# Four edits to a streaming-encoder layer with a mixture of experts: gathered rows spread over both partition halves, router products ahead of a gathered column, tile sums and additions interleaved, the output gain spread by products

## The chip, the cores and the metric

One core of a Trainium2 chip runs the whole program. Times are microseconds (us) on the device; the metric is the time of the whole program. Engines are called PE (TensorE), DVE (VectorE), ACT (ScalarE), POOL (GpSimd) and SP (SyncE, which here only issues DMAs). Sixteen DMA engines serve the core.

## What is computed

```
h = rmsnorm(concat(meta_tokens, x)); u = h @ w_in            # 16 + 512 rows of 1024
y = concat(conv_module(u), windowed_attention(u), hgrn2(u))
h_res = concat(meta_tokens, x) + y @ w_out
x2 = rmsnorm(h_res)                                          # ffn_norm
g = argmax(x2 @ w_rg + b_rg)                                 # 1 of 4 groups
e1, e2 = top2((x2 @ w_re + b_re)[group g])                   # 2 of its 8 experts, weights w1, w2
moe = sum over e in (e1, e2) of w_e * (silu(x2 @ w_gate[e]) * (x2 @ w_up[e])) @ w_down[e]
out = rmsnorm(h_res + moe)[16:]                              # final_norm, output (1, 512, 1024)
```

There are 32 experts. The three matrices of one expert are 1 MB each in float32, so the experts' weights alone are 96 MB.

## The kernel before, in words

The program is written engine by engine; semaphores order them. It has two stages. The mixer stage (to about 275 us) makes h_res for four tiles of 128 tokens. Its end interleaves the output projection with the router: `project` (L1516) makes a tile half, `router_turn` (L1524) turns 128x128 blocks of it, `router` (L1532) multiplies them with the router's weights, and DVE's `residual` (L953), `router_half` (L967, copies the turned half) and `select` (L985 to L1029) choose the experts. Line L960 writes the normed rows.

The expert stage works on **columns**: up to 128 rows of tokens, gathered by one indirect DMA into 128 partitions (`rows_in`, L2115), and scattered to `expert_out` by another one when their results are there (`rows_out`, L2121). A column holds one to four experts. `rows_plan` (L52) lays them out: six experts with low numbers start early ("early" columns, and "rest" columns for their rows of the last tile), the others are sorted by their count into heavy (one expert in 128 rows), mid (two in 64 rows each) and light columns (four in 32 rows each). Each part is a **block**: 42 in all. A block is gate and up products (L1628 for 64 rows, L1636 for 32), a silu on ACT (L1775, L1777), a product on DVE, a transposition (L1642, L1645), down products (L1651, L1659), and copies to `yb` by ACT and DVE (L1864 and others). `turn_x` (L1621) turns a gathered column for the products. PE's order is written out by block number in `experts_tensor`, DVE's in `experts_vector`.

SP loads the weights into a ring of seven slots, three DMAs an expert (L438, L441, L448), each issued when the products that read the slot are done. `places` (L1194) works out the row of each token in its column from a code word: two bits give the quarter (`rq`) at which its block starts, and `from_end` (quarters 1 and 2) says that the rows are counted down from the block's end:

```
mark(V.tensor_tensor(from_end, low_q, high_q, ALU.not_equal))
mark(V.tensor_scalar(row_r, cq, 32.0, -1.0, ALU.mult, ALU.add))
mark(V.scalar_tensor_tensor(out=row_r, in0=rq, scalar=64.0, in1=row_r, op0=ALU.mult, op1=ALU.add))
```

The index of a row that no token has lies beyond the bounds, and nothing is moved for it. With the given inputs the router's choices give these columns, in the order of the plan (counted from the reference's own top-2 choices; p is the partition):

| column | rows in p 0-63 | in p 64-127 |
|---|---|---|
| rest 13 | 19 | 0 |
| mid 4, light 8 | 36, 55 | 45, 49 |
| heavy 0, heavy 1 | 64, 64 | 22, 5 |
| light 9, heavy 2 | 46, 59 | 30, 0 |
| mid 5, heavy 3 | 36, 55 | 35, 0 |
| mid 6, mid 7 | 34, 30 | 32, 28 |
| light 11, light 10 | 5, 28 | 0, 17 |

Rest 12 is not gathered but picked from the last tile by products, and the last column, light 10, is not scattered: its results go into the sum by eight products (`last_rows`, L2009) whose weights `mix_flat` are made at blocks 20 to 25.

At the end (`rows_back`, L1689 and L1691) SP waits for all scatters and reads back, tile by tile, the residual rows and two expert rows for each token, 512 KB each. DVE's `two_rows` (L1903) adds the two weighted expert rows of a tile; then eight additions (L1913, two a tile) add the products of the last column; ACT squares and sums a tile (L1828), and `row_norm` (L1934) scales it. `gain_out` holds final_norm in all 128 partitions: POOL loads it with a broadcasting DMA (L2149) after the scatter of column number 9 of the plan. It cannot come sooner, since `slot_is` uses that memory until `last_rows` (L1258) has made `mix`.

## Time and profile before

| | |
|---|---|
| median of 3 runs | 553.11 us (552.26 to 555.14) |
| profiled execution, its own time | 553.58 us |
| its span | 551.7 us |
| PE busy, PE weight loads | 501.0 us (91%), 320.2 us (58%) |
| DVE, ACT, POOL busy | 255.5 us (46%), 154.1 us (28%), 39.0 us (7%) |
| moved by DMA | 146.71 MB, mean 266 GB/s |
| chain that ended last | PE 72%, DMA 16%, DVE 4%, SP's queue 4% |

The share of busy time is an average over two stages with different limits, so it has to be read by stretches. A DMA share slightly over 1 means that all 16 engines are occupied all the time.

### The profile page before, as it was taken

To read this page: it belongs to the slowest core of one execution; us is meant where nothing else is said; L and a number is where in the kernel's file an instruction comes from. 1 tells how busy PE (TensorE), PEld (TensorE's weight loads), DVE (VectorE), ACT (ScalarE), POOL (GpSimd) and SP (SyncE) were. 2 spreads that over 40 slices of the span, in tenths; PEclk is the share of its full clock that TensorE was granted. 3 is DMA by queue.
4 is the path that set the end of the run, shared out by engine and by line. 5 is a ranking of instruction groups with operands and counts; after the bars stand their busy time and mean duration, and the time that the engine had idled before them with its cause. 6 is when DMAs were issued, how large, how long until landed. Compare 5 with 4: busy or idle time off the path is not lost.

```text
span 551.7 us, 11100 instructions
## 1 busy us (share of the span) xinstructions
PE 501.0 (91%) x4585; PEld 320.2 (58%) x4585; DVE 255.5 (46%) x638; ACT 154.1 (28%) x380; POOL 39.0 (7%) x46
## 2 busy tenths in 40 slices
PE   5999999999999999999899999999999799776660
PEld 4886468885556655557566656565565455443420
DVE  3205995868245864626456333342442122131167
ACT  5410003766013622422123322231222111120124
POOL 0010000000001000000110011211111111000000
PEclk8899999999999999999979999999999899786885
DMA  8990000000006799607968899999999999999943
GB/s 268 363 350 3 1 0 2 0 1 1 2 1 215 266 421 410 264 39 266 400 229 337 351 407 336 414 413 418 417 413 413 417 416 416 420 416 411 404 166 152
DMA packets 38947, 146.71 MB, mean 266 GB/s; under 512 B 5151, under 2 KB 12565, under 8 KB 30320
## 3 DMA queue, kind: packets, MB, share of 16 engines
q1 hardware_dynamic: 32736, 134.18, 62.1%
q0 software_dynamic: 5616, 11.36, 5.6%
q8 instruction: 37, 0.61, 0.4%
q10 hardware_dynamic: 544, 0.44, 0.2%
q14 instruction: 14, 0.11, 0.1%
HBM read 135.83 MB, written 18.87 MB: 280 GB/s over the span
## 4 chain that ended last, share of the span: by engine, by line
PE 72%; DMA 16%; DVE 4%; SPq 4%; issue 1%; ACT 0%; DVEq 0%; POOLq 0%; ACTq 0%
PE bank L1628 10%; PE bank L1516 9%; PE bank L1347 6%; PE bank L1381 5%; DMA area_w<-in_w_exp_up 5%; PE bank L1349 5%; PE bank L1636 5%; PE bank L1651 5%; DMA area_x<-in_w_exp_up 4%; PE bank L1339 4%; DMA area_g<-expert_out 3%; PE bank L1460 3%; PE bank L1282 3%; PE bank L1621 2%; PE bank L1659 2%; PE bank L1423 2%
## 5 line engine op out<-in xcount | busy, mean ns | idle before, releaser
L1516 PE MATMUL bank<-area_w,area_m 128*128 128x512 f32 x128 | 56.7, 594 | 0.4 <-issue 0.4
L1628 PE MATMUL bank<-area_w,area_m 128*64 128x256 f32 x320 | 41.1, 403 | 3.3 <-DMA area_w<-in_w_exp_up 3.3
L785 DVE SCALAR_TENSOR_TENSOR area_m<-area_g,cols,area_m 128x512 f32<-128x512 f32 x60 | 39.8, 746 | 0.0
L1516 PEld LDWEIGHTS bank<-area_w,area_m 128*128 128x128 f32 x128 | 23.6, 190 | 26.9 <-issue 26.9
L1347 PE MATMUL bank<-area_h,area_w 128*128 128x264 f32 x160 | 35.9, 386 | 0.0
L1628 PE MATMUL bank<-area_g,area_m 128*64 128x256 f32 x256 | 32.8, 400 | 3.3 <-DMA area_g<-in_w_exp_up 3.3
L1628 PEld LDWEIGHTS bank<-area_w,area_m 128*64 128x64 f32 x320 | 23.0, 145 | 19.5 <-issue 9.8
L1347 PEld LDWEIGHTS bank<-area_h,area_w 128*128 128x128 f32 x160 | 30.4, 190 | 5.6 <-issue 0.5
L1381 PE MATMUL bank<-area_h,area_w 128*128 128x512 f32 x64 | 30.8, 612 | 0.0
L1846 DVE COPY cst<-bank 128x128 f32<-128x128 f32 (+1 forms) x38 | 9.9, 261 | 40.2 <-PE bank L1642 30.0
L1349 PE MATMUL bank<-area_h,area_w 128*128 128x512 f32 x64 | 27.6, 592 | 0.0
L1628 PEld LDWEIGHTS bank<-area_g,area_m 128*64 128x64 f32 x256 | 18.0, 142 | 15.8 <-issue 7.7
L1636 PE MATMUL bank<-area_g,area_m 128*32 128x128 f32 x640 | 23.2, 291 | 3.3 <-DMA area_g<-in_w_exp_up 3.3
L1864 DVE COPY area_m<-bank 64x512 f32<-64x512 f32 x20 | 13.9, 694 | 21.9 <-PE bank L1651 21.9
L1636 PEld LDWEIGHTS bank<-area_g,area_m 128*32 128x32 f32 x640 | 18.7, 117 | 8.8 <-issue 7.2
L1621 PE MATMUL bank<-cst,area_h 128*128 128x128 f32 x136 | 21.1, 305 | 2.4 <-DMA area_h<-normed,cols 2.4
L1636 PE MATMUL bank<-area_w,area_m 128*32 128x128 f32 x576 | 20.7, 291 | 2.9 <-DMA area_w<-in_w_exp_up 2.8
L1855 DVE TENSOR_TENSOR cst<-cst,bank 64x128 f32<-64x128 f32 x20 | 5.9, 293 | 37.0 <-ACT cst L1777 36.8
L1739 ACT ACTIVATE area_m<-bank 128x512 f32<-128x512 f32 x17 | 10.2, 598 | 44.2 <-PE bank L1621 39.7
L2121 POOL DMA_INDIRECT expert_out<-area_m,cst x13 | 12.9, 994 | 126.8 <-DVE area_m L1864 80.7
L1636 PEld LDWEIGHTS bank<-area_w,area_m 128*32 128x32 f32 x576 | 16.4, 116 | 8.9 <-issue 7.8
L1853 DVE TENSOR_TENSOR cst<-cst,bank 128x128 f32<-128x128 f32 x22 | 6.4, 290 | 32.6 <-ACT cst L1775 30.6
(382 smaller groups left out, 819.9 us busy)
## 6 DMA issues: line engine op xcount, KB each, us to landing
area_w<-in_w_exp_gate SPq DMA_DIRECT2D x14, 1024.0 KB
area_w<-in_w_exp_up SPq DMA_DIRECT2D x14, 1024.0 KB
area_g<-in_w_exp_gate SPq DMA_DIRECT2D x14, 1024.0 KB
area_g<-in_w_exp_up SPq DMA_DIRECT2D x14, 1024.0 KB
area_g<-in_w_exp_down SPq DMA_DIRECT2D x14, 1024.0 KB, 21.9
area_w<-in_w_exp_down SPq DMA_DIRECT2D x14, 1024.0 KB, 17.6
area_w<-in_w_in SPq DMA_DIRECT2D x7, 1024.0 KB, 12.6
area_w<-in_w_out SPq DMA_DIRECT2D x2, 2048.0 KB, 12.7
```

What stands on the lines that cost most here:

```text
L785: ins = V.scalar_tensor_tensor(out=mixT[:, i, :], in0=src, scalar=w, in1=mixT[:, i, :], op0=ALU.mult, op1=ALU.add)
L1282: ins = T.matmul(half_of(n, h), w_in_sb[:, k, COL[n]:COL[n] + P], hT[:, k, h * HALF:(h + 1) * HALF], start=(k == 0), stop=(k == KT - 1))
L1339: ins = T.matmul(out_b[:, n0:n0 + w], hT[:, k, t0:t0 + P], w_in_sb[:, k, c0:c0 + w], start=(k == 0), stop=(k == KT - 1))
L1347: ins = T.matmul(half_of(n, h), w, hT[:, k, h * HALF:(h + 1) * HALF], start=(k == 0), stop=(k == KT - 1))
L1349: ins = T.matmul(out_b[:, :], w, hT[:, k, META:], start=(k == 0), stop=(k == KT - 1))
L1381: ins = T.matmul(bank[QUERY_BANK[i]][:, :], w_in_sb[:, k, C_Q + i * P:C_Q + (i + 1) * P], hT[:, k, META:], start=(k == 0), stop=(k == KT - 1))
L1460: ins = T.matmul(bank[2 + n % 2][s, t], kk, qq, start=True, stop=True)
L1516: ins = T.matmul(bank[7][:, :], mixT[:, k, j * P:(j + 1) * P], w_out_sb[:, n, k, :], start=(k == 0), stop=(k == KT - 1))
L1621: ins = T.transpose(bank[2 + k // 4][:, (k % 4) * P:(k % 4 + 1) * P], cols_of[:, k, :], ident)
L1628: ins = T.matmul(out_b[h * BC:(h + 1) * BC, 0:2 * P], x[:, k, :], w_gate_up[slot][:, :, k, h * P:(h + 1) * P], start=(k == 0), stop=(k == ...
L1636: ins = T.matmul(out_b[q * 32:(q + 1) * 32, 0:P], x[:, k, :], w_gate_up[slot][:, q // 2, k, q % 2 * P:(q % 2 + 1) * P], start=(k == 0), st ...
L1651: ins = T.matmul(out_b[n * BC:(n + 1) * BC, :], aT[:, f * BC:(f + 1) * BC], w_down[slot][:, f, n * 512:(n + 1) * 512], start=(f == 0), sto ...
```

## The change

Four edits, independent of each other:

1. **Rows over both halves.** The two blocks of rest column 13 start at partitions 0 and 64 instead of 0 and 32 (`rest_row`). And in columns with an odd number the sense of `from_end` is turned over, with two small DVE operations in `places`: heavy 1 then has its rows in 5/64 (p 0-63/p 64-127) instead of 64/5, heavy 3 in 0/55 instead of 55/0, rest 13 in 13/6 instead of 19/0. The counts by half of all others stay; within the halves the odd columns' rows begin at the other end of their blocks.
2. **Router.** The last four router products of the last tile (and one product whose result nothing reads, `fill`) come before the wait for the first gathered column and its `turn_x`.
3. **Sum.** DVE adds tile j-1's products of the last column behind tile j's `two_rows`, instead of all eight additions behind all the sums.
4. **Gain.** POOL loads final_norm into partition 0 alone; PE spreads it by two products with a row of ones (`gain_spread`, at blocks 34 and 35) into bank 7, and DVE copies it to `gain_out` (`gain_taken`, one turn later).

```diff
+def rest_row(c, n):
+    return (ROWS_B, BC)[c] * n
...
-    rest = [("late" if c else "picked", AT_REST + c, [(p, ROWS_B * n, ROWS_B) for n, p in enumerate(ps)]) for c, ps in enumerate(REST)]
+    rest = [("late" if c else "picked", AT_REST + c, [(p, rest_row(c, n), ROWS_B) for n, p in enumerate(ps)]) for c, ps in enumerate(REST)]
...
+GAIN_AT = 34
...
+                mark(V.tensor_scalar(odd_col, word, 14, 1, ALU.logical_shift_right, ALU.bitwise_and))
...
+                mark(V.tensor_tensor(from_end, from_end, odd_col, ALU.not_equal))
...
+            def gain_taken(h):
+                dve.wait_ge(mix_turned, 2 + h)
+                V.tensor_copy(gain_out[:, h * 512:(h + 1) * 512], bank[7][:, :]).then_inc(mix_ready, 1)
...
+            fill(bank[4], 1)
+            pe.wait_ge(hfT_v, 5)
+            router(3, bank[6], range(4, KT)).then_inc(logits, 1)
             pe.wait_ge(d_xg[0], 16)
             turn_x(T, xg[0]).then_inc(xT_made, 1)
-            pe.wait_ge(hfT_v, 5)
-            router(3, bank[6], range(4, KT)).then_inc(logits, 1)
...
+                if GAIN_AT < b_ <= GAIN_AT + 2:
+                    gain_taken(b_ - 1 - GAIN_AT)
...
-            for j in range(NT):
-                two_rows(j, w_rest, 16 + 48, 0)
-            for j in range(NT):
+            def own_rows(j):
                 for n in range(2):
                     dve.wait_ge(mixed, 2 * j + n + 1)
                     h = xs[:, j, n * 512:(n + 1) * 512]
                     V.tensor_tensor(h, h, bank[MIX_BANK[j][n]][:, :], ALU.add).then_inc(summed, 1)
+            two_rows(0, w_rest, 16 + 48, 0)
+            for j in range(1, NT):
+                two_rows(j, w_rest, 16 + 48, 0)
+                own_rows(j - 1)
+            own_rows(NT - 1)
...
-                    dve.wait_ge(d_gain, 32)
+                    dve.wait_ge(mix_ready, 3)
...
+            def gain_spread(h):
+                pe.wait_ge(d_gain, 32)
+                pe.wait_ge(mix_ready, 1 + h)
+                T.matmul(bank[7][:, :], cst[0:1, K_ONE:K_ONE + P], gain_out[0:1, h * 512:(h + 1) * 512],
+                         start=True, stop=True).then_inc(mix_turned, 1)
...
+                if GAIN_AT <= b_ < GAIN_AT + 2:
+                    gain_spread(b_ - GAIN_AT)
...
-                    Q.dma_start(gain_out, final_norm.rearrange("(a d) -> a d", a=1).to_broadcast([P, D])).then_inc(d_gain, 16)
+                    Q.dma_start(gain_out[0:1, :], final_norm.rearrange("(a d) -> a d", a=1)).then_inc(d_gain, 16)
```

On PE at the border of the two stages (128x36: router products; cst,area_x: turning the residual; cst,area_h: turning the gathered column; area_w,area_m 64x256: gate and up products of the first block), before:

```order
L1532 MATMUL bank<-cst 128x36 x4
L1524 MATMUL bank<-cst,area_x 128x128 x4
L1621 MATMUL bank<-cst,area_h 128x128 x8
L1532 MATMUL bank<-cst,area_m 128x36 x4
L1628 MATMUL bank<-area_w,area_m 64x256 x16
```

and now (lines of the changed file):

```order
L1546 MATMUL bank<-cst 128x36 x4
L1538 MATMUL bank<-cst,area_x 128x128 x4
L1303 MATMUL bank<-cst 128x256
L1546 MATMUL bank<-cst,area_m 128x36 x4
L1636 MATMUL bank<-cst,area_h 128x128 x8
L1643 MATMUL bank<-area_w,area_m 64x256 x16
```

The four router products have passed the eight transpositions, and a product of 128x256 stands between.

On DVE at the end of the program (area_w and area_g hold the expert rows, bank the products of the last column), before:

```order
L1903 SCALAR_TENSOR_TENSOR area_x<-area_w,cst,area_x 128x1024
L1903 SCALAR_TENSOR_TENSOR area_x<-area_g,cst,area_x 128x1024
L1913 TENSOR_TENSOR area_x<-area_x,bank 128x512 x8
L1915 COMPARE_AND_BRANCH
```

and now, from the third tile on:

```order
L1920 SCALAR_TENSOR_TENSOR area_x<-area_w,cst,area_x 128x1024
L1920 SCALAR_TENSOR_TENSOR area_x<-area_g,cst,area_x 128x1024
L1929 TENSOR_TENSOR area_x<-area_x,bank 128x512 x2
L1920 SCALAR_TENSOR_TENSOR area_x<-area_w,cst,area_x 128x1024
L1920 SCALAR_TENSOR_TENSOR area_x<-area_g,cst,area_x 128x1024
L1929 TENSOR_TENSOR area_x<-area_x,bank 128x512 x4
L1937 COMPARE_AND_BRANCH
```

Behind the last pair of sums stand four additions instead of eight.

On PE at blocks 34 and 35 the spreading products stand behind the down products of the block before:

```order
L1666 MATMUL bank<-area_g,cst 64x512 x4
L2028 MATMUL bank<-gain_out,cst 128x512
L1651 MATMUL bank<-area_w,area_m 32x128 x16
L1657 MATMUL bank<-cst 128x128
```

The second of them waits for DVE's copy of the first, and the products of the next block (L1651) are queued behind it.

## Rows read from the trace of the kernel before

**Rows 1.** Windows of the expert stage: start:end length, busy us (x instructions) by engine, PEclk, DMA share, GB/s.
```profile
350.00:400.00 50.00, 50.00 (x679) 30.35 (x679) 18.38 (x46) 12.20 (x30) 8.06 (x8) 1.00 1.02 415
400.00:450.00 50.00, 46.06 (x494) 27.49 (x488) 15.08 (x37) 10.12 (x25) 8.68 (x9) 0.97 1.02 415
450.00:500.00 50.00, 42.12 (x444) 24.58 (x442) 12.11 (x28) 8.77 (x20) 4.96 (x5) 0.90 1.02 416
500.00:525.00 25.00, 14.86 (x251) 10.27 (x243) 4.24 (x12) 4.07 (x13) 0.00 (x0) 0.73 1.02 408
```
**Rows 2.** Timeline, PE: start, us, line, tiles, count, [idle before, what ended it].
```profile
437.43 3.25 PE L1628 MATMUL bank<-area_w,area_m 128*64 128x256 f32 x16 [3.33 <-DMA area_w<-in_w_exp_up]
471.93 3.68 PE L1628 MATMUL bank<-area_g,area_m 128*64 128x256 f32 x16 [3.28 <-DMA area_g<-in_w_exp_up]
487.60 1.71 PE L1636 MATMUL bank<-area_x,area_m 128*32 128x128 f32 x32 [2.13 <-DMA area_x<-in_w_exp_up]
518.34 3.42 PE L1636 MATMUL bank<-area_g,area_m 128*32 128x128 f32 x64 [2.75 <-DMA area_g<-in_w_exp_up]
```
**Rows 3.** Timeline, SP: one weight DMA, start and time that the issue took.
```profile
459.44 3.40 SPq L438 DMA_DIRECT2D area_x<-in_w_exp_gate  x1
```
**Rows 4.** Windows of the last transfers' end, columns as in rows 1.
```profile
524.00:525.00 1.00, 0.11 (x4) 0.00 (x0) 0.37 (x1) 0.79 (x3) 0.00 (x0) 1.00 1.05 422
525.00:536.00 11.00, 8.59 (x16) 3.60 (x16) 7.40 (x7) 1.99 (x3) 0.00 (x0) 0.84 0.43 173
530.00:536.00 6.00, 4.45 (x11) 1.71 (x9) 3.66 (x4) 0.00 (x0) 0.00 (x0) 1.00 0.31 126
530.00:531.00 1.00, 1.00 (x4) 0.52 (x3) 1.00 (x1) 0.00 (x0) 0.00 (x0) 1.00 0.45 184
```
**Rows 5.** Timeline of the end: sums, products of the last column, additions, squares, scaling.
```profile
524.63 1.28 DVE L1903 SCALAR_TENSOR_TENSOR area_x<-area_w,cst,area_x 128x1024 f32<-128x1024 f32 x1 [2.24 <-DMA area_g<-expert_out]
525.87 8.59 PE L2009 MATMUL bank<-area_m,cst 128*128 128x512 f32 x16 [1.75 <-ACT area_m L1760]
532.19 1.28 DVE L1903 SCALAR_TENSOR_TENSOR area_x<-area_w,cst,area_x 128x1024 f32<-128x1024 f32 x1 [1.16 <-DMA area_g<-expert_out]
535.94 1.28 DVE L1903 SCALAR_TENSOR_TENSOR area_x<-area_w,cst,area_x 128x1024 f32<-128x1024 f32 x1 [1.15 <-DMA area_g<-expert_out]
538.58 4.87 DVE L1913 TENSOR_TENSOR area_x<-area_x,bank 128x512 f32<-128x512 f32 x8
544.72 1.04 ACT L1828 ACTIVATE area_w<-area_x 128x1024 f32<-128x1024 f32 x1
543.37 4.99 DVE L1934 SCALAR_TENSOR_TENSOR area_x<-area_x,stat,gain_out 128x1024 f32<-128x1024 f32 x5
```
**Rows 6.** Timeline at the border of the stages: PE, DVE, ACT.
```profile
274.61 0.69 DVE L967 COPY area_m<-bank 128x512 f32<-128x512 f32 x1 [0.75 <-PE bank L1524]
276.99 1.97 PE L1621 MATMUL bank<-cst,area_h 128*128 128x128 f32 x8 [2.42 <-DMA area_h<-normed,cols]
278.76 1.76 PE L1532 MATMUL bank<-cst,area_m 128*128 128x36 f32 x8
279.50 0.59 ACT L1743 ACTIVATE area_m<-bank 128x512 f32<-128x512 f32 x1
280.45 4.96 PE L1628 MATMUL bank<-area_w,area_m 128*64 128x256 f32 x32
285.34 0.22 PE L1948 MATMUL bank<-cst 128*32 128x1 f32 x2
```
**Rows 7.** Windows there, columns as in rows 1.
```profile
276.27:283.10 6.83, 6.11 (x30) 4.91 (x32) 2.19 (x11) 1.08 (x2) 0.00 (x0) 0.50 0.87 306
283.10:286.51 3.41, 3.41 (x34) 2.37 (x32) 2.67 (x15) 1.87 (x4) 0.38 (x1) 1.00 0.07 28
```
**Rows 8.** DMA issues by line: engine, count, KB, median us to landing.
```profile
gain_out<-in_final_norm POOLq DMA_DIRECT2D x1, 512.0 KB, 11.7
```
**Rows 9.** Timeline: a copy from a bank by DVE near block 35.
```profile
481.37 0.69 DVE L1864 COPY area_m<-bank 64x512 f32<-64x512 f32 x1 [1.11 <-PE bank L1651]
```

More of the change, by code:

```diff
@@ L112 @@
 FROM_END = slice(1, 3)
+assert PLAN[PICKED][1] % 2 == 0
 FAR = 8192
@@ L359, in trunk @@
         n_extra = cut(cst, NE).bitcast(I32)
-        word, rk, cq, rq, bq, fq, over_by, over_blk, beyond, low_q, high_q, from_end = \
-            (cut(cst, 2 * NT).bitcast(I32).rearrange("p (k j) -> p k j", k=2) for _ in range(12))
+        word, rk, cq, rq, bq, fq, over_by, over_blk, beyond, low_q, high_q, odd_col, from_end = \
+            (cut(cst, 2 * NT).bitcast(I32).rearrange("p (k j) -> p k j", k=2) for _ in range(13))
         row_r = cut(cst, 2 * NT).rearrange("p (k j) -> p k j", k=2)
@@ L1035, in build_codes @@
                     for n, e in enumerate(ps):
-                        mark(V.memset(code[:, e:e + 1], float((ROWS_B // 32 << 9) + (n << 12) + (AT_REST + c << 14) + ROWS_B - ROWS_A)))
+                        mark(V.memset(code[:, e:e + 1], float((ROWS_B // 32 << 9) + (rest_row(c, n) // 32 << 12) + (AT_REST + c << 14) + ROWS_B - ROWS_A)))
                 step(V.memset(cap, 32.0))
@@ L1266, in last_rows_turned @@
                 V.tensor_copy(mix_flat, bank[7][:, :]).then_inc(mix_ready, 1)
-            return sort_in, order, experts, words, places, index, spare_in, spares, last_rows, last_rows_turned
+            def gain_taken(h):
+                dve.wait_ge(mix_turned, 2 + h)
+                V.tensor_copy(gain_out[:, h * 512:(h + 1) * 512], bank[7][:, :]).then_inc(mix_ready, 1)
+            return sort_in, order, experts, words, places, index, spare_in, spares, last_rows, last_rows_turned, gain_taken
         def mixer_tensor(pe):
@@ L1284, in half_product, with fill @@
                 return ins
-            def fill(n):
+            def fill(b, n):
                 for _ in range(n):
-                    T.matmul(bank[1][:, 0:2 * P], ident, cst[:, 0:2 * P], start=True, stop=True)
-            fill(4)
+                    T.matmul(b[:, 0:2 * P], ident, cst[:, 0:2 * P], start=True, stop=True)
+            fill(bank[1], 4)
             turn_tile(0)
@@ L1299, in mixer_tensor @@
             ins.then_inc(metaT, 1)
-            fill(3)
+            fill(bank[1], 3)
             pe.wait_ge(d_win[0], 16)
@@ L1834, in experts_scalar, with experts_vector @@
             act.dma_start(out[0, ET * P:, D // 2:], xs[:, ET, D // 2:]).then_inc(d_out, 16)
-        def experts_vector(dve, sort_in, order, experts, words, places, index, spare_in, spares, last_rows, last_rows_turned):
+        def experts_vector(dve, sort_in, order, experts, words, places, index, spare_in, spares, last_rows, last_rows_turned, gain_taken):
             V = nc.vector
@@ L2000, in last_rows_turned @@
                 ins.then_inc(mix_turned, 1)
+            def gain_spread(h):
[3 more added lines that the diff above has]
+                         start=True, stop=True).then_inc(mix_turned, 1)
             def last_rows():
-                pe.wait_ge(mix_ready, 1)
+                pe.wait_ge(mix_ready, 3)
                 pe.wait_ge(y_lo, NB)
```

## The prediction

> **What bounds the kernel now.** I read the windows of the expert stage first [rows 1]. The reader is to see that two limits follow each other. From 350 to 400 PE is busy for all 50.00 us. From 400 to 525 it is idle for 3.9 + 7.9 + 10.1 = 21.9 us, while the DMA share stays at 1.02: all sixteen DMA engines are occupied, at 408 to 416 GB/s. The timeline of PE shows what ended its longer waits: weights, for 3.33, 3.28, 2.13 and 2.75 us [rows 2]. SP's timeline tells the same from the other side: an issue takes 3.40 us, so the rings are full, and no slot is what SP waits for [rows 3]. So until about 355 us PE sets when a slot is free and a load can start, and from then on it is the number of bytes on the slowest DMA engine.
>
> The slowest engine is the point. In the last windows of the transfers [rows 4] the share is 1.05 at 524 and only 0.45 at 530, with nothing new being issued that could wait. 0.45 / 1.02 x 16 is 7 engines: about half of them still have work when the other half has finished. The last expert rows start DVE's last sum at 535.94 [rows 5]. The work left at 525.0 is 0.43 x 11 us of all engines; shared evenly it would take 0.43 x 11 / 1.02 = 4.6 us and end at 529.6.
>
> Behind it stands DVE: two sums of a tile (1.28 us each), eight additions (4.87), five scalings (4.99), then the last store [rows 5].
>
> **Edit 1, rows over both halves.** The table of columns, counted from heavy 0 on (its gather, and all scatters that are still to come then), gives 924 row transfers for p 0-63 and 415 for p 64-127; with the edit it is 690 and 649. I take a half of the partitions to be served by a half of the engines, since that is what the step to 7 engines looks like. One engine then has (924 - 415) / 8 = 64 transfers more than one of the other half, afterwards 5. From [rows 4] the two groups can be separated: 0.31 x 6 us x 16 / 1.02 = 29 engine-us lie behind 530.0 and belong to the late group, and with 8 engines for the 5 us before that it has some 68, which is 8.5 each, so it ends at 533.5 in the mean; the early group at about 525.8. That is 7.7 us for 64 rows, 0.12 us a row, where a transfer at full rate (4 KB at 416/16 = 26 GB/s) would take 0.157 [rows 1]; some of the lag is lost in DMA pauses before 350. The lower end: only the halves are levelled, and the last engine stays 2.4 us behind the mean of its group. Last landing 529.6 + 0.3 + 2.4 = 532.3, a gain of 3.6 us. The upper end: all engines level, 535.9 - 529.6 = 6.3. The odd columns also start at the other end of their blocks, so engines within a half should come closer too; I take **4.7 us**. All of it reaches the end, because weights, the last products and the rows read back all wait for the slowest engine.
> The Trainium skill (DMA: Bandwidth & Descriptors, The descriptor swizzle) says the same more finely: engines 0 to 7 write partitions 0-63 and 8 to 15 write 64-127, in groups of four partitions. Counted by its formula, the fullest engine has 134 transfers before and 94 after with a mean of 84, which at 0.12 us is an estimate of 4.8 us. The step at 530 agrees with the halves; no row shows the groups of four.
> The two operations in `places` are small ones, and before 300 us DVE is not what PE waits for: **0.1 us** at most.
>
> **Edit 4, gain.** The broadcasting DMA writes 512 KB [rows 8] at a time when the DMA engines are the limit [rows 1]: 512 KB / 416 GB/s = **1.3 us** for all of them; 0 is the lower end. What it adds: each spreading product is 128x512, and the eight such products for the last column take 8.59 us, 1.07 a product, partly at the low clock [rows 5]. The second also waits for DVE: the copy of the block's results, 0.69 us, which follows PE's last down product [rows 9], and the copy of the gain, which I price like that one, 0.69. PE thus stands some 1.4 us and works 2.1, 3.5 in all, at blocks 34 and 35 (470 to 483). Queued behind it is the next block's gate and up, and behind that the scatter of the last but one column. I cost it at **nothing**: PE idles 21.9 us between 400 and 525, and edits 1 and 4 use up 6.0. If that cover were gone, it would be 3.5. The new wait for the small load has from 418 to 470 us against 11.7 to landing [rows 8].
>
> **Edit 2, router.** PE stands from 274.57 to 276.99 for the gathered column [rows 6]; DVE's copy that the router products need is there at 275.3. Now they and the unread product fill most of that hole. Router's 1.76 us leave the path ahead of the first block: `turn_x` 276.95, ACT's two copies (from the end of `turn_x` at 278.96 to 280.09 here, 1.1 us), so the first block starts near 279.3 to 280.2 instead of 280.45. The logits come some 4 us sooner, but PE does not ask for their outcome before the block is done, at 285.34: on PE's own order only the 0.2 to 1.1 us count. The clock is the larger part. It is granted at 0.50 (1.2 GHz) from 276.27 to 283.10, right behind the standstill, and 1.00 (2.4 GHz) afterwards [rows 7]. The block takes 4.96 us, 2.65 of it at the low level; at 2.4 GHz throughout it would be 3.6. With the low clock gone: 276.95 + 1.1 + 1.1 + 0.1 + 3.6 = 282.9, a gain of 2.4. With nothing changed in the clock: 0.2. ACT's copies leave a new hole of 1.2 us ahead of the block, so the clock may fall all the same, a little later: I take **1.2 us**. It passes to the end through the slots: loads start when PE frees them, until about 355, and from there the whole DMA chain stands earlier.
>
> **Edit 3, sum.** Before, from the last sum's start to the end of the additions: 2.6 + 4.9 = 7.5 us. Now four of the eight additions stand before the last pair: a tile's rows land 3.75 us apart (532.19, 535.94), the pair takes 2.6, two additions 1.2, which is 3.8 and just fits. Left are 2.6 + 4 x 0.61 = 5.05, and 0.1 of slip: a gain of **2.3 us**. The squares on ACT end 2 us ahead of their use and stay out of it: the last needs 1.8 us, three scalings 3.6. Ends: 0, if the products of the last column (525.87 to 534.46) were late, and 2.45.
>
> **The sum.** 1.2 + 4.7 + 1.3 + 2.3 - 0.1 = 9.4 us. The profiled execution took 553.6, which gives 544.2; from the median, 0.5 below it, it would be 543.7. Forecast **544.0 us**.
>
> **The rivals.**
> A. *Levelling does nothing.* The late half has another cause, or a transfer with rows in one half is shared by all engines anyway. For it: the trace names no engine. Against it: heavy 0 to 3, all in the lower half, explain the size of the lag. It gives 544.2 + 4.7 = 549 us. Chance 0.12.
> The Trainium skill (DMA: Bandwidth & Descriptors, in its list of what to do) has a rule on this side: two transfers to disjoint partition halves both spray over all 16 engines. By it 549 would be the outcome; here each transfer has 128 rows of which some are void, and the 7 engines at 530 speak against the rule.
> B. *PE's new stand becomes the bound.* With weights 6 us earlier the waits at 437 and 472 vanish first, and the 3.5 us at blocks 34 and 35 come where little is left. For it: the waits before 480 are 6.6 us in all. Against: three waits follow, the last 2.75 at 518 [rows 2]. It gives up to 544.2 + 3.5 = 547.7. Chance 0.12.
> C. *Slower: DVE held behind the last column's products.* `own_rows(0)` stands ahead of the third sum and waits for the first product pair (525.87 + 8.59/4 = 528.0), where before nothing but the additions did. It has 3 us of slack: DVE is through with two pairs of sums at 532.19 - 1.16 = 531.0. If the last block came later than that by more than 3 us, each further us would count, with 2 x 2.6 + 6 x 0.6 = 8.9 us of DVE work behind it. From a lateness of 3 + 9.4 it is slower than before; at 16 us it would be 557. Nothing in the profile is near that. Chance 0.02.
> A and B together would be 552.4, no change to measure: 0.04.
> Forecast's own case: 0.70.
>
> **How the numbers follow.** The range reaches down to all upper ends (2.4 - 1.2 for the clock, 1.6 for levelling, 0.15): 541.0, and up past A with the clock not regained: 549.5. Within 0.5% (2.8 us, about what a measurement of this kernel can tell) means above 550.3: A and B together, and half of what is worse than B. Faster 0.93, same 0.05, slower 0.02.
>
> **What the next profile would show.** The share in the last windows of the transfers falls from 1.0 to near 0 within 3 us, not 10 (edit 1); were 0.45 still there for 5 us, A holds. PEclk stays at 1.00 around 277 to 283, or falls for a shorter time, and the first block starts before 280. Behind DVE's last pair of sums stand four additions, 2.4 us. The load of `gain_out` is 4 KB, PE's wait at block 35 is followed by a shorter wait for weights. The forecast is wrong if PE's idle time between 400 and 525 falls under 5 us.

## The result, and the profile after

| | before | after |
|---|---|---|
| median of 4 runs | 553.20 us (552.26 to 555.14) | 547.15 us (544.30 to 548.22) |
| profiled execution, its own time | 553.58 us | 547.10 us |
| its span | 551.7 us | 545.3 us |
| ratio of the times | | 0.9878 (95%: 0.9832 to 0.9924) |

The kernel is 6.05 us faster by the medians and 6.5 by the profiled executions. The forecast was a gain of 9.4 us and a time of 544.0 us. The direction and the range were right; a third of the gain is missing.

The page of the kernel after gives its engines and queues. q0 is POOL's queue of gathers, scatters and small loads.

```profile
PE 502.3 (92%) x4591; PEld 319.2 (59%) x4591; DVE 257.0 (47%) x642; ACT 154.1 (28%) x380; POOL 38.9 (7%) x46
...
DMA packets 38836, 146.19 MB, mean 268 GB/s; under 512 B 5168, under 2 KB 12582, under 8 KB 30209
...
q0 software_dynamic: 5504, 10.84, 5.5%
```

PE is busy 1.3 us longer, and 146.71 - 146.19 = 0.52 MB are gone: the broadcast of the gain.

The windows of the kernel after (columns as in [rows 1]) answer to [rows 1] and [rows 4]:

```profile
400.00:450.00 50.00, 49.73 (x539) 29.62 (x534) 16.69 (x41) 10.69 (x26) 8.65 (x9) 1.00 1.02 415
450.00:500.00 50.00, 40.06 (x435) 23.05 (x435) 13.26 (x30) 8.90 (x21) 4.93 (x5) 0.92 1.02 417
...
524.00:525.00 1.00, 1.00 (x2) 0.41 (x2) 0.71 (x1) 0.00 (x0) 0.00 (x0) 0.50 1.00 397
525.00:526.00 1.00, 1.00 (x2) 0.34 (x1) 0.96 (x2) 0.00 (x0) 0.00 (x0) 0.50 0.93 373
526.00:527.00 1.00, 1.00 (x3) 0.42 (x2) 0.96 (x2) 0.00 (x0) 0.00 (x0) 0.81 0.92 373
527.00:528.00 1.00, 1.00 (x3) 0.38 (x2) 1.00 (x2) 0.00 (x0) 0.00 (x0) 1.00 0.82 332
528.00:529.00 1.00, 1.00 (x4) 0.47 (x3) 1.00 (x2) 0.76 (x1) 0.00 (x0) 1.00 0.58 234
529.00:530.00 1.00, 1.00 (x4) 0.29 (x2) 0.96 (x2) 0.89 (x4) 0.00 (x0) 1.00 0.28 115
530.00:531.00 1.00, 0.36 (x1) 0.00 (x0) 0.97 (x2) 0.00 (x0) 0.00 (x0) 1.00 0.12 49
```

The shelf at 0.45, on which half of the engines worked alone, is gone. The share falls from 0.92 in the window from 526 to 527 to 0.12 in that from 530 to 531. PE now idles 0.3 us between 400 and 450 where it was 3.9. From 450 to 500 it idles 9.9; the DMA engines stay full.

The timeline of DVE at the end, kernel after, answers to [rows 5]:

```profile
520.37 1.28 DVE L1920 SCALAR_TENSOR_TENSOR area_x<-area_w,cst,area_x 128x1024 f32<-128x1024 f32 x1 [3.65 <-DMA area_g<-expert_out]
...
524.29 1.28 DVE L1920 SCALAR_TENSOR_TENSOR area_x<-area_w,cst,area_x 128x1024 f32<-128x1024 f32 x1 [1.31 <-DMA area_g<-expert_out]
...
528.13 1.27 DVE L1920 SCALAR_TENSOR_TENSOR area_x<-area_w,cst,area_x 128x1024 f32<-128x1024 f32 x1
...
531.96 1.27 DVE L1920 SCALAR_TENSOR_TENSOR area_x<-area_w,cst,area_x 128x1024 f32<-128x1024 f32 x1
...
534.59 2.48 DVE L1929 TENSOR_TENSOR area_x<-area_x,bank 128x512 f32<-128x512 f32 x4
```

The third and the fourth tile (528.13, 531.96) begin without a bracket, straight behind two additions of the tile before: their rows lie ready, and DVE itself is the limit from there. Behind the last pair of sums stand four additions of 2.48 us in place of eight.

PE at the border of the stages, kernel after, answers to [rows 6]:

```profile
275.99 0.66 PE L1538 MATMUL bank<-cst,area_x 128*128 128x128 f32 x4
...
277.43 1.08 PE L1546 MATMUL bank<-cst,area_m 128*128 128x36 f32 x8 [0.35 <-DVE area_m L974]
...
278.35 1.12 PE L1636 MATMUL bank<-cst,area_h 128*128 128x128 f32 x8
...
280.69 5.30 PE L1643 MATMUL bank<-area_w,area_m 128*64 128x256 f32 x32 [1.22 <-ACT area_m L1754]
...
285.92 0.22 PE L1970 MATMUL bank<-cst 128*32 128x1 f32 x2
```

The wait of 2.42 us for the gathered column is gone, but the first block takes 5.30 us, longer than before (4.96). The windows there, which answer to [rows 7], say why:

```profile
276.00:280.60 4.60, 3.12 (x22) 2.52 (x22) 2.46 (x10) 2.70 (x6) 0.00 (x0) 1.00 0.97 315
280.60:284.00 3.40, 3.31 (x16) 2.22 (x18) 3.04 (x16) 1.39 (x3) 0.00 (x0) 0.50 0.95 308
```

The clock falls to 1.2 GHz later and for half as long, but still inside the block: it falls at 280.6, at the end of a new hole of 1.22 us.

Three marks split the change of the span: the products behind the first block (285.34 before, 285.92 after; I call them the mark at the border), the first sum (524.63, 520.37) and the first scaling (543.37, 536.99). The stretches before, between and behind them changed by +0.58, -4.84, -2.12 and 0.0, together -6.4 us. The forecast had -1.1, -6.0 and -2.3.

### The profile page after: what moved, and what is told of

The parts are those of the page before. It is cut to its first block, busy times and chain, and to the rows that moved or that the text cites. A ratio compares the mean times of both kernels' runs of the same rounds, so it can differ in the third digit from the quotient of the medians.

```text
span 545.3 us, 11118 instructions
## 1 busy us (share of the span) xinstructions
PE 502.3 (92%) x4591; PEld 319.2 (59%) x4591; DVE 257.0 (47%) x642; ACT 154.1 (28%) x380; POOL 38.9 (7%) x46
## 2 busy tenths in 40 slices
DMA packets 38836, 146.19 MB, mean 268 GB/s; under 512 B 5168, under 2 KB 12582, under 8 KB 30209
## 4 chain that ended last, share of the span: by engine, by line
PE 76%; DMA 10%; DVE 6%; SPq 5%; issue 1%; ACT 0%; DVEq 0%; POOLq 0%; ACTq 0%
PE bank L1530 10%; PE bank L1643 10%; PE bank L1361 7%; PE bank L1651 6%; PE bank L1395 5%; PE bank L1363 5%; PE bank L1666 5%; DMA area_g<-in_w_exp_up 5%; PE bank L1353 4%; DMA area_g<-expert_out 3%; PE bank L1296 3%; PE bank L1474 3%; PE bank L1674 3%; PE bank L1636 3%; SPq L445 2%; PE bank L1437 2%
## 5 line engine op out<-in xcount | busy, mean ns | idle before, releaser
L1530 PE MATMUL bank<-area_w,area_m 128*128 128x512 f32 x128 | 58.3, 608 | 0.4 <-issue 0.4
L1361 PEld LDWEIGHTS bank<-area_h,area_w 128*128 128x128 f32 x160 | 30.4, 190 | 5.6 <-issue 0.5
L1651 PE MATMUL bank<-area_g,area_m 128*32 128x128 f32 x640 | 22.8, 286 | 3.4 <-DMA area_g<-in_w_exp_up 3.4
L1651 PE MATMUL bank<-area_w,area_m 128*32 128x128 f32 x576 | 21.9, 303 | 3.8 <-DMA area_w<-in_w_exp_up 3.8
L1651 PEld LDWEIGHTS bank<-area_g,area_m 128*32 128x32 f32 x640 | 18.2, 115 | 8.7 <-issue 7.3
L1651 PEld LDWEIGHTS bank<-area_w,area_m 128*32 128x32 f32 x576 | 17.3, 122 | 10.0 <-issue 8.9
L1353 PE MATMUL bank<-area_w,area_h 128*128 128x128 f32 (+1 forms) x128 | 21.3, 327 | 0.0
L1363 PEld LDWEIGHTS bank<-area_h,area_w 128*128 128x128 f32 x64 | 12.2, 190 | 14.9 <-issue 14.8
```

The source lines that it names most:

```text
L1353: ins = T.matmul(out_b[:, n0:n0 + w], hT[:, k, t0:t0 + P], w_in_sb[:, k, c0:c0 + w], start=(k == 0), stop=(k == KT - 1))
L1361: ins = T.matmul(half_of(n, h), w, hT[:, k, h * HALF:(h + 1) * HALF], start=(k == 0), stop=(k == KT - 1))
L1363: ins = T.matmul(out_b[:, :], w, hT[:, k, META:], start=(k == 0), stop=(k == KT - 1))
L1530: ins = T.matmul(bank[7][:, :], mixT[:, k, j * P:(j + 1) * P], w_out_sb[:, n, k, :], start=(k == 0), stop=(k == KT - 1))
L1651: ins = T.matmul(out_b[q * 32:(q + 1) * 32, 0:P], x[:, k, :], w_gate_up[slot][:, q // 2, k, q % 2 * P:(q % 2 + 1) * P], start=(k == 0), st ...
```

## The experiments

Three sets, each on one chip with runs of the kernel before beside it. Intervals are 95%. "To the sum" is the time from the mark at the border to DVE's first sum, "sums" that from the first sum to the first scaling, both from the profiled execution. The ratios are estimates with their intervals, not the quotients of the medians beside them.

| kernel | median us (runs) | before beside it (runs) | ratio | span | to the sum | sums |
|---|---|---|---|---|---|---|
| rows_alone | 547.51 (12) | 550.98 (35) | 0.9954 (0.9930 to 0.9978) | 543.5 | 235.34 | 18.85 |
| sum_alone | 549.39 (12) | the same | 0.9973 (0.9944 to 1.0002) | 544.7 | 239.26 | 16.48 |
| gain_alone | 550.38 (12) | the same | 0.9987 (0.9958 to 1.0016) | 546.8 | 238.03 | 18.75 |
| router_alone | 552.22 (12) | the same | 1.0017 (0.9993 to 1.0040) | 547.4 | 239.67 | 18.74 |
| before_again | 552.63 (1) | 553.14 (11) | | 550.8 | 239.86 | 18.75 |
| after_again | 546.46 (6) | the same | 0.9883 (0.9842 to 0.9924) | 544.8 | 233.97 | 16.74 |
| rows_dealt | 545.16 (6) | the same | 0.9885 (0.9841 to 0.9930) | 542.3 | 233.79 | 16.62 |
| fill_more | 543.50 (6) | the same | 0.9856 (0.9809 to 0.9903) | 541.3 | 234.51 | 16.59 |
| dealt_fill | 543.40 (6) | 550.87 (23) | 0.9870 (0.9834 to 0.9906) | 539.6 | 232.93 | 17.47 |
| fill_only | 551.66 (12) | the same | 1.0002 (0.9973 to 1.0031) | 552.5 | 240.62 | 18.77 |
| after_less_router | 544.62 (6) | the same | 0.9874 (0.9833 to 0.9914) | 543.4 | 234.97 | 16.61 |
| after_less_rows | 549.44 (12) | the same | 0.9977 (0.9947 to 1.0007) | 547.0 | 237.41 | 17.11 |
| kernel before | | | | 551.7 | 239.29 | 18.74 |
| kernel after | | | | 545.3 | 234.45 | 16.62 |

Runs of one kernel spread over some 4 us and more, so a ratio alone does not weigh a part of 1 or 2 us. The two stretches repeat within 0.6 us in executions of the same kernel (239.29 and 239.86; 234.45 and 233.97), so the verdicts on the parts go by them. A base of 239.3 to 239.9 is taken for kernels without edits 1 and 4; only fill_only's 240.62 stands out from it.

**rows_alone**, edit 1 alone on the kernel before:

```diff
+    return (ROWS_B, BC)[c] * n
...
+                mark(V.tensor_tensor(from_end, from_end, odd_col, ALU.not_equal))
```

> The kernel before with edit 1 alone. Theory (a half of the partitions is served by a half of the DMA engines): the share of the DMA engines stays near 1 to about 528 and falls to nothing within 4 us, the last sum starts 3.5 us earlier than in the kernel before (4.7 if the engines within a half come closer as well), and the program ends 3.5 to 4.7 us earlier. Rival (the halves share all engines): the share still stands at 0.45 for 5 us, and the time is the one before.

Windows of rows_alone, last transfers:

```profile
520.00:521.00 1.00, 1.00 (x3) 0.46 (x2) 0.75 (x1) 0.00 (x0) 0.00 (x0) 0.66 1.01 401
521.00:522.00 1.00, 1.00 (x4) 0.44 (x3) 0.96 (x2) 0.00 (x0) 0.00 (x0) 1.00 0.98 393
522.00:523.00 1.00, 1.00 (x3) 0.38 (x2) 0.85 (x1) 0.00 (x0) 0.00 (x0) 1.00 0.99 389
523.00:524.00 1.00, 1.00 (x4) 0.50 (x3) 0.00 (x0) 0.00 (x0) 0.00 (x0) 1.00 0.78 307
524.00:525.00 1.00, 1.00 (x4) 0.45 (x3) 0.94 (x1) 0.00 (x0) 0.00 (x0) 1.00 0.70 283
525.00:526.00 1.00, 1.00 (x3) 0.19 (x1) 0.96 (x2) 0.00 (x0) 0.00 (x0) 1.00 0.55 225
526.00:527.00 1.00, 0.18 (x1) 0.00 (x0) 0.67 (x1) 0.00 (x0) 0.00 (x0) 1.00 0.27 111
```

The shelf goes with this edit alone. The shares from 520 on add up to 5.28, which is 5.2 us of all engines at 1.02; the last transfer ends near 527.1, so the last engine is 7.1 - 5.2 = 1.9 us behind the mean of all. I call this distance the lag. In the kernel before the transfers end near 535.4, half a microsecond ahead of DVE's last sum at 535.94:

```profile
535.00:536.00 1.00, 0.00 (x0) 0.00 (x0) 0.06 (x1) 0.00 (x0) 0.00 (x0) 1.00 0.04 16
```

The lag before is thus 10.4 - 0.43 x 11 / 1.02 = 5.8 us [rows 4]. Taken the same way from windows of 0.2 us, it is 5.7 to 6.8 in the seven profiles without edit 1 and 2.0 (rows_alone) to 2.9 (after_less_router) in the five that have it and nothing dealt. To the sum: 239.3 to 239.9 becomes 235.3, which is 4.0 to 4.5 us.

**sum_alone**, edit 3 alone:

```diff
+            for j in range(1, NT):
+                two_rows(j, w_rest, 16 + 48, 0)
+                own_rows(j - 1)
+            own_rows(NT - 1)
```

> The kernel before with edit 3 alone. Theory: the last landing does not move, DVE goes through four additions in its gaps, and the program ends 2.3 us earlier (range 1.8 to 2.45). Rival (the products of the last column hold the additions, and these hold the sums): less than 1 us, and DVE stands waiting for PE L2009 in front of an addition.

DVE of sum_alone:

```profile
519.98 1.28 DVE L1903 SCALAR_TENSOR_TENSOR area_x<-area_w,cst,area_x 128x1024 f32<-128x1024 f32 x1 [2.11 <-DMA area_g<-expert_out]
...
527.60 1.28 DVE L1903 SCALAR_TENSOR_TENSOR area_x<-area_w,cst,area_x 128x1024 f32<-128x1024 f32 x1
...
536.46 4.99 DVE L1939 SCALAR_TENSOR_TENSOR area_x<-area_x,stat,gain_out 128x1024 f32<-128x1024 f32 x5
```

First sum to first scaling is 16.48 where the old order takes 18.74 to 18.85 in six executions: 2.3 us. The third sum already starts without a wait here. Everything ahead is as before (239.26).

**gain_alone**, edit 4 alone:

```diff
-                    Q.dma_start(gain_out, final_norm.rearrange("(a d) -> a d", a=1).to_broadcast([P, D])).then_inc(d_gain, 16)
+                    Q.dma_start(gain_out[0:1, :], final_norm.rearrange("(a d) -> a d", a=1)).then_inc(d_gain, 16)
```

> The kernel before with edit 4 alone. Theory: 512 KB less in a stretch in which all DMA engines are occupied, 1.3 us earlier at the end; the 3.5 us that PE stands and works longer at blocks 34 and 35 are taken out of its wait for weights at about 485 and cost nothing. Rival: PE's stand delays the last scatter and what follows, so 0 to 2 us are lost instead.

PE of gain_alone at blocks 34 and 35:

```profile
467.09 1.95 PE L1633 MATMUL bank<-area_g,area_m 128*64 128x256 f32 x16 [2.11 <-DMA area_g<-in_w_exp_up]
...
475.40 1.64 PE L2013 MATMUL bank<-gain_out,cst 1*128 1x512 f32 x2 [1.61 <-DVE gain_out L1271]
```

PE stands 1.61 us for DVE's copy, and the spreading takes 1.64 and, ahead of it at 463.86, 1.12: 4.4 us. PE still waits for weights behind each of them, 2.11 us at 467.09 and 3.67 us at 498.42, so there is idle time to take them from. Still the first sum comes at 238.03, 1.3 to 1.8 us sooner. The bytes are gained, and PE's stand costs nothing.

**router_alone**, edit 2 alone:

```diff
+            T.matmul(bank[4][:, 0:2 * P], ident, cst[:, 0:2 * P], start=True, stop=True)
+            pe.wait_ge(hfT_v, 5)
+            router(3, bank[6], range(4, KT)).then_inc(logits, 1)
             pe.wait_ge(d_xg[0], 16)
             turn_x(T, xg[0]).then_inc(xT_made, 1)
```

> The kernel before with edit 2 alone. Theory: PE's products of counts start 1.2 us earlier against the last router_turn than before (0.2 if the clock is low as long as before, 2.4 if it is not low at all), and the program ends by as much earlier. Rival: it is all lost in DVE's and PE's order behind it, 0 us.

PE of router_alone at the border:

```profile
274.76 1.16 PE L1622 MATMUL bank<-cst,area_h 128*128 128x128 f32 x8 [0.56 <-DMA area_h<-normed,cols]
277.14 3.67 PE L1629 MATMUL bank<-area_w,area_m 128*64 128x256 f32 x32 [1.22 <-ACT area_m L1740]
280.75 0.22 PE L1949 MATMUL bank<-cst 128*32 128x1 f32 x2
```

In this one profile the clock does not fall at the border (the block takes 3.67 us), which looks like the full gain. But the times do not show it: 1.0017 (0.9993 to 1.0040) leaves a gain of at most 0.4 us. To see why, the profiles of all kernels can be put side by side. "Hole" is PE's idle time ahead of the gathered column and ahead of the first block; "low" is how long 1.2 GHz was granted, in the mixer between 253 and 262 and at the border between 274 and 285. "Turn" is the last `router_turn` (its start).

| executions | order | low in the mixer | hole ahead of column | ahead of block | low at the border | column to mark | turn to mark |
|---|---|---|---|---|---|---|---|
| before, before_again | old | none | 2.42, 2.40 | none | 6.8, 6.8 | 8.35, 8.33 | 11.4, 11.4 |
| rows_alone, sum_alone, after_less_router | old | 3.4 each | 0.61, 0.45, 0.63 | 0.40, 0.40, 0.41 | none | 5.98 each | 7.2, 7.1, 7.3 |
| gain_alone | old | 6.8 | none | 0.29 | none | 5.93 | 6.4 |
| router_alone | new | none | 0.56 | 1.22 | none | 5.99 | 9.1 |
| after, after_again | new | 3.4, 3.4 | none | 1.22, 1.22 | 3.4, 3.4 | 7.57, 7.57 | 9.9, 9.9 |
| rows_dealt | new | none | 0.43 | 1.22 | 3.4 | 7.68 | 10.6 |
| after_less_rows | new | none | 0.41 | 1.22 | 6.8 | 8.82 | 11.8 |
| fill_more, dealt_fill | new, filled | none | 0.47, 0.35 | 0.36, 0.35 | none | 5.98, 5.98 | 9.0, 8.9 |
| fill_only | old, filled | 3.4 | none | 0.41 | none | 5.87 | 8.1 |

Three things stand in it. At full clock both orders take 5.98 from `turn_x` to the mark: in the old order the router products fill PE's time while ACT copies the turned column, so moving them only trades one hole for another. A low clock at the border begins inside a hole or right behind it in both: the 2.4 us in the old order, which are there only where the column comes late, and the 1.22 us in the new one, in 4 of 5 executions. And by these profiles what edit 2 is worth depends on when the column comes. Where it comes late (no low clock in the mixer), PE has 2.4 us to fill, and the time from turn to mark goes from 11.4 to 9.1, 10.6 or 11.8. Where it comes early (a low clock in the mixer), the router products now hold `turn_x` up: it starts 2.4 us behind the last `router_turn` in place of 0.5 to 1.3, and the time from turn to mark rises to 9.9, from 6.4 in gain_alone and 7.1 to 7.3 in the other three.

**before_again**, the kernel before with no edit, to see which marks repeat.

> The kernel before once more, for its profile: where the clock falls at the border of the stages, and how long PE waits for the gathered column. Theory (the low clock at 276 to 283 was this execution's own): in a second execution it stands elsewhere, and the first block takes 3.6 us in place of 4.9. Rival (it is what the standstill of 2.4 us brings every time): again low for some 7 us from 276 on.

PE of before_again at the border, and then its windows there:

```profile
275.56 1.97 PE L1621 MATMUL bank<-cst,area_h 128*128 128x128 f32 x8 [2.40 <-DMA area_h<-normed,cols]
...
279.01 4.95 PE L1628 MATMUL bank<-area_w,area_m 128*64 128x256 f32 x32
```

```profile
274.80:281.60 6.80, 6.04 (x28) 4.86 (x30) 2.13 (x11) 1.09 (x2) 0.00 (x0) 0.50 0.87 313
```

The rival holds: the standstill and the low clock are there again, as is the time to the sum (239.86).

**after_again**, the kernel after with no edit.

> The changed kernel once more. Theory (the edits add up: 4.0 for the rows, 1.35 for the gain, 2.3 for the sum, 0 for the router): 7 us faster than before, ratio 0.987. Rival (they overlap): ratio 0.993, the sum of what the four alone were timed at.

It gives 0.9883 (0.9842 to 0.9924), to the first result's 0.9878. The theory's 0.987 lies inside the interval, and the rival's 0.993 just outside it: the parts add up. Its clock is low from 280.4 to 283.8, the first block takes 5.29 us, and the third and fourth sums start without a wait, all as in the first profile.

**rows_dealt**, the kernel after, with the 32 rows of each quarter dealt in steps of four partitions. It tries whether engines within a half can be levelled further:

```diff
-                        V.tensor_tensor(slot_is[:, k, j:j + 2, :], cst[:, K_IOTA:K_IOTA + P].unsqueeze(1).to_broadcast([P, 2, P]),
+                        V.tensor_tensor(slot_is[:, k, j, :].rearrange("p (g l h) -> p g h l", g=4, l=8),
+                                        cst[:, K_IOTA:K_IOTA + P].rearrange("p (g h l) -> p g h l", g=4, l=8),
```

> The changed kernel with the rows of each block of 32 partitions dealt out in steps of four (rank 0 to partition 0, rank 1 to partition 4 and so on; four more DVE operations in places). If engines serve groups of four partitions, the fullest has 89 transfers instead of 94, and the last landing comes 0.6 us earlier. If the 2.6 us by which the last engine ends behind the mean of all come from the rows within a half, 2 us earlier. If the halves are all that counts, no change.

Windows of rows_dealt:

```profile
523.00:524.00 1.00, 1.00 (x3) 0.48 (x2) 0.96 (x2) 0.00 (x0) 0.00 (x0) 0.50 0.98 381
524.00:525.00 1.00, 1.00 (x4) 0.48 (x3) 1.00 (x2) 0.00 (x0) 0.00 (x0) 0.92 0.87 344
525.00:526.00 1.00, 1.00 (x4) 0.41 (x3) 1.00 (x2) 0.74 (x1) 0.00 (x0) 1.00 0.73 295
526.00:527.00 1.00, 1.00 (x4) 0.39 (x3) 0.96 (x2) 0.91 (x4) 0.00 (x0) 1.00 0.54 221
527.00:528.00 1.00, 1.00 (x4) 0.37 (x2) 0.96 (x2) 0.00 (x0) 0.00 (x0) 1.00 0.27 111
```

The shares from 523 to 528 add up to 3.39, 3.3 us of all engines, and the last transfer ends near 528.1, so the lag is 1.8 us, to 2.6 in the kernel after (4.67 / 1.02 = 4.6 of 7.2 us from 524 on). But rows_alone has 1.9 without any dealing, and dealt_fill, with it, 2.4, as has fill_more without. The time to the sum is 0.2 to 0.7 shorter than in its fellows. That dealing levels anything is not shown.

**fill_more**, the kernel after with two unread products behind `turn_x`, in the hole of 1.22 us:

```diff
             turn_x(T, xg[0]).then_inc(xT_made, 1)
+            fill(bank[4], 2)
```

> The changed kernel with two more unread products of 128x256 between turn_x and the first block, 0.9 us of the 1.2 us in which PE stands for ACT's copies. Theory (a hole there is what lowers the clock): PEclk stays at 1.00 from 276 to 285, the first block takes 3.6 us, 1.7 us earlier than the changed kernel where that had the low clock. Rival (the clock falls by what lies before, or not at all): no change.

PE of fill_more:

```profile
275.94 1.16 PE L1637 MATMUL bank<-cst,area_h 128*128 128x128 f32 x8 [0.47 <-DMA area_h<-normed,cols]
276.93 1.03 PE L1303 MATMUL bank<-cst 128*128 128x256 f32 x4
278.32 3.67 PE L1644 MATMUL bank<-area_w,area_m 128*64 128x256 f32 x32 [0.36 <-issue]
```

The block starts 2.38 us behind `turn_x`, no later than without the fill (2.34 in the kernel after), and takes 3.67 instead of 5.30. The median is 3.0 us below after_again on the same chip (543.50 to 546.46), though the intervals of the ratios overlap. That the hole is what lowers the clock is likely and not shown: it stayed high in two of two executions with the fill, and in one of five without.

**dealt_fill**, both of these:

```diff
+            fill(bank[4], 2)
...
+                        V.tensor_tensor(slot_is[:, k, j, :].rearrange("p (g l h) -> p g h l", g=4, l=8),
```

> The changed kernel with both additions, rows dealt in steps of four and two more unread products between turn_x and the first block. Theory: PEclk 1.00 at the border, products of counts 6.0 us behind turn_x, last landing 1.6 us behind the mean of all engines; 2.5 us faster than the changed kernel. Since DVE is the bound behind the second tile's rows, of the dealing only what moves the second tile counts, 0.3 to 0.6 us; rival: all of the 0.65.

DVE of dealt_fill:

```profile
522.40 1.28 DVE L1923 SCALAR_TENSOR_TENSOR area_x<-area_w,cst,area_x 128x1024 f32<-128x1024 f32 x1 [0.76 <-DMA area_g<-expert_out]
```

It has the shortest span, 539.6 us, and 543.4 us in the median, as fill_more. Its first sum comes 1.0 to 1.6 us sooner behind the mark than in the kernels with the four edits and no dealing, but 0.76 of that is lost again in the wait for the third tile: of the dealing 0.7 us are left at the first scaling, against fill_more (250.40 to 251.10 behind the mark), one execution each.

**fill_only**, the kernel before with four unread products ahead of the wait for the column and nothing else, to price the clock apart from the order:

```diff
+            for _ in range(4):
+                T.matmul(bank[4][:, 0:2 * P], ident, cst[:, 0:2 * P], start=True, stop=True)
             pe.wait_ge(d_xg[0], 16)
```

> The kernel before, its order kept, with four unread products of 128x256 in the standstill ahead of turn_x. Theory (the order of the router's products is worth nothing, the clock is all): no low clock between 270 and 285, products of counts 6.0 us behind turn_x, where the profiles of the kernel before with the standstill of 2.4 us have 8.3; 1 us faster than before in the median, since part of its executions have the high clock there anyway. Rival (the order matters): behind turn_x still 1.5 us more than with edit 2.

PE of fill_only:

```profile
281.25 3.67 PE L1630 MATMUL bank<-area_w,area_m 128*64 128x256 f32 x32 [0.41 <-issue]
```

The clock stays at 2.4 GHz through the block, and yet the ratio to the kernel before is 1.0002 (0.9973 to 1.0031). The forecast gain of 1 us is not seen, though the interval does not rule it out. The profile caught an execution in which the column came early: here the four unread products hold `turn_x` up, which starts 2.2 us behind the last `router_turn` (276.77 to 278.99) where the other profiles of the old order with an early column have 0.5 to 1.3. So the fills cost 1 us or more there and could gain only where the column comes late; no profile shows that case.

**after_less_router**, the kernel after without edit 2 (the old order, no fill):

```diff
-            fill(bank[4], 1)
-            pe.wait_ge(hfT_v, 5)
-            router(3, bank[6], range(4, KT)).then_inc(logits, 1)
             pe.wait_ge(d_xg[0], 16)
             turn_x(T, xg[0]).then_inc(xT_made, 1)
+            pe.wait_ge(hfT_v, 5)
+            router(3, bank[6], range(4, KT)).then_inc(logits, 1)
```

> The changed kernel with edit 2 undone. Theory (edit 2 is worth at most 0.8 us, and only where the clock would be low): 0 to 0.8 us slower than the changed kernel, ratio to before 0.988 to 0.990. Rival (my step, 1.2 us or more): 0.990 to 0.992.

0.9874 (0.9833 to 0.9914), where the whole change has 0.9878 and 0.9883. No loss is seen; the interval is too wide to exclude the rival's 0.990 by itself.

**after_less_rows**, the kernel after without edit 1:

```diff
-                mark(V.tensor_tensor(from_end, from_end, odd_col, ALU.not_equal))
```

> The changed kernel with edit 1 undone. Theory: the share stands at 0.45 again for 4 to 5 us, from the products of counts to the first sum it takes 238 us instead of 234, and it is 4 us slower than the changed kernel. Rival (PE's new stand at blocks 34 and 35 had eaten part of edit 1): less than 3 us slower.

Windows of after_less_rows:

```profile
525.00:526.00 1.00, 1.00 (x3) 0.48 (x2) 0.00 (x0) 0.00 (x0) 0.00 (x0) 0.55 0.49 201
526.00:527.00 1.00, 1.00 (x3) 0.42 (x3) 0.99 (x1) 0.00 (x0) 0.00 (x0) 1.00 0.44 180
...
529.00:530.00 1.00, 1.00 (x4) 0.42 (x3) 1.00 (x3) 0.03 (x1) 0.00 (x0) 1.00 0.46 188
```

The shelf is back, and most of the gain is gone: 0.9977 (0.9947 to 1.0007). The time to the sum is 237.41 where the kernels with all four edits and no dealing have 233.97 to 234.51: 2.9 to 3.4 us. Another 0.4 to 0.5 us lie behind it, in the wait for the second tile ("sums" is 17.11 where those have 16.59 to 16.74), so edit 1 is worth 3.4 to 3.8 us at the first scaling. The theory's 4 us is nearer than the rival's less than 3.

## Why the prediction was right or wrong

**What bounds the kernel: right.** A late half of the DMA engines ends the transfers; the shelf at 0.45 goes and comes with edit 1 alone. Rival A is refuted by rows_alone and after_less_rows. The rule of the Trainium skill that was weighed there (DMA: Bandwidth & Descriptors, Rules for kernel authors) does not carry over to this case, transfers of 128 rows of which some are void.

**Edit 1, 4.7 us: mis-sized, 2.9 to 4.5.** It is 4.0 to 4.5 us alone, 3.5 to 4.1 in the presence of edit 4 (238.03 against 233.97 to 234.51), 2.9 to 3.4 in the presence of the others, each taken to the first sum. The step that failed is "engines within a half should come closer too; I take 4.7". The lag is still 2.6 us in the kernel after, and 2.0 to 2.9 in its fellows; the prediction's lower end assumed just that, 2.4, and gave 3.6. Its upper end, 6.3 for all engines level, took DVE's start at 535.94 for the end of the transfers; they end near 535.4, and 5.8 was the most that levelling could give. By the count of 134 to 94 transfers from the Trainium skill (DMA: Bandwidth & Descriptors, The descriptor swizzle) the estimate was 4.8 us. The same count gives a lag before of (134 - 84) x 0.12 = 6.0 us, an estimate that the measured 5.7 to 6.8 bear out, but 1.2 afterwards where 2.0 to 2.9 are measured. Some lag is thus not made by the counts of rows; what makes it stays open.

**Edit 4, 1.3 us: right.** Alone it gives 1.3 to 1.8. PE's stand is 1.61 us and its spreading 1.12 and 1.19 in the kernel after, 3.9 in all where 3.5 were forecast, and the cover held. Rival B is refuted: gain_alone is faster to the sum by the full gain, and in the kernel after PE still idles 18.5 us between 400 and 525 (0.3, 9.9 and 8.3), where the bound for a failure was 5.

**Edit 2, 1.2 us: wrong, no gain.** router_alone leaves it at most 0.4 us, and after_less_router sees no loss without it. The failed step has two halves. "The first block starts near 279.3 to 280.2": ACT's copies, not the router products, set the distance to `turn_x`; it is 2.38 us at full clock in both orders (275.03 to 277.41 in rows_alone, 274.76 to 277.14 in router_alone). Where the column comes early, the products even hold `turn_x` up by 1 us and more. And "ACT's copies leave a new hole of 1.2 us, so the clock may fall all the same, a little later: I take 1.2": with the hole it is low in 4 of 5 executions, for 3.4 or 6.8 us, which costs 1.6 to 2.8. The old order has a low clock at the border only where the column comes 2.4 us late, in 2 of 6. I took the standstill and the clock of one execution for properties of the kernel. From the turn to the mark edit 2 then gains 2.3 and 0.8 us or loses 0.3 where the column comes late (11.4 to 9.1, 10.6, 11.8), and loses 2.7 or more where it comes early (7.1 to 7.3, once 6.4, to 9.9).

**What stood ahead of the border** was in no term. PE reaches the last `router_turn` at 275.99 instead of 273.92, though PE's code there is the same. Windows of the kernel after and of the kernel before in the mixer:

```profile
256.70:260.10 3.40, 3.40 (x7) 1.70 (x7) 3.36 (x28) 0.00 (x0) 0.53 (x1) 0.50 1.02 417
```

```profile
256.70:260.10 3.40, 3.40 (x9) 1.49 (x9) 3.40 (x32) 0.00 (x0) 0.53 (x1) 1.00 1.01 364
```

3.4 us at half the clock cost 1.7. A stretch of 3.4 or 6.8 us that begins between 253.9 and 257.6 is low in 7 of 14 executions, among them kernels that change nothing ahead of the border (sum_alone, gain_alone, fill_only); so it does not need the change. Another stretch of 6.8 us, from 10 or 11 us on, is low in 4 of 14: in the kernels before and after alike, not in before_again, and in this pair it about cancels. PE is 2.1 us later at the last `router_turn` in this pair of profiles, 0.4 of it unexplained, and from there to the mark 1.5 of that come back (11.4 to 9.9). That last figure is no gain of edit 2: the kernel before was caught with the column late, the kernel after with it early. How often the stretches are low in the unprofiled runs, and so what share of the medians they hold, is open.

**Edit 3, 2.3 us: right,** 2.1 to 2.3. Not forecast: "which is 3.8 and just fits" is the point at which DVE becomes the bound. A tile needs 3.84 us of it (524.29, 528.13, 531.96), the rows came 3.75 apart, so from the third tile on what the DMA engines gain is not seen. Rival C, DVE held behind the last column's products, did not show: those begin at 520.19, and no addition waits.

**The sum.** From profile to profile: 3.5 for edit 1 and 1.3 for edit 4 (4.84 together, 6.0 forecast), 2.1 for edit 3, and up to the mark a loss of 0.6 instead of a gain of 1.1. 9.4 - 1.2 - 0.2 - 1.7 = 6.3, the 6.4 us of the spans up to rounding: 1.2 are missing in the levelling, 0.2 in DVE's tail and 1.7 up to the mark. The last part mixes edit 2 with where the clock was low in the two profiles. The experiments show no gain for edit 2, and the other parts alone, 3.5 + 1.3 + 2.1 = 6.9, are what the medians show, 6.05 and, in after_again, 6.7.

## What to carry to other kernels

When the DMA share falls to a shelf near a half at the end of a long full stretch, count the rows of gathers and scatters by half of the partitions, and move rows, not bytes: here that is the largest part of the gain, for two small DVE operations. A product that is moved to fill one of PE's holes leaves the place it had covered; look at both before pricing it. And price a hole or a clock only from several executions of the same code: here the late column that edit 2 was to make use of is there in 7 of 14 executions only.

## What the runs showed of the hardware

- The granted clock differs between executions of the same instructions. Ahead of the stretch at 256.7 PE was busy all the time in both kernels (6.70 of 6.70 us, mostly products of 36 columns); it fell to 1.2 GHz in the one and not in the other.
- At the border it fell inside or right behind idle times of 1.22 us in four of five executions, and not where two unread products of 128x256 filled them (two executions). Two against five is too few to call the hole the cause.
- Half of the DMA engines can stand idle while the others work on rows of the other half: shares of 0.44 to 0.49 for 5 us in after_less_rows, and of 0.44 to 0.47 for 5 us in the kernel before and in gain_alone, and no such shelf in any kernel with edit 1.
- Time lost to a low clock ahead of a gather can come back in part. Where the mixer had its low stretch, the gathered column lands 3.6 to 3.8 us after POOL issues the gather's second part (three executions; 273.77 to 277.58 in after_less_router), elsewhere 5.4 to 5.6 (seven; 271.38 to 276.99 in the kernel before). Why the later gather is the faster one is not shown. In the old order each of the six executions without fills had one of the two low stretches, in the mixer or at the border, and none both; the kernel after had both in both of its profiles.
